# Hyena long convolution by folded half-length transforms, with the modulation sums moved to GpSimd

## The chip, the cores and the metric

The kernel runs on one core of a Trainium2 chip. The metric is the device time of one launch in microseconds; lower is better. The profile is one execution of the same program, taken by the hardware profiler.

## The reference

Two transformer-like blocks are applied to a latent sequence of 512 positions and 1024 features, all in float32. Only the first block is touched by the change. Cut to what matters:

```python
mod_x = silu(c) @ w_mod + b_mod            # 6 x 1024 values for the latent sequence
mod_c = silu(c_ctx) @ w_mod + b_mod        # the same for the context (only shift and scale are used)
hx = modulate(rmsnorm(x), sh_a, sc_a)
hc = modulate(rmsnorm(ctx), csh_a, csc_a)
q, k, v, hy = split(hx @ w_in)             # attention and Hyena inputs
attn = differential_attention(q, [k_ctx, k], [v_ctx, v])

def hyena_filters(L):                      # 2 orders x 2 directions x 512 channels
    h = MLP_with_sines(positions) * exp(-t * deltas)
    k_full = concat([h_forward, 0, reversed(h_backward[1:])])
    return rfft(k_full)                    # length 2 L

def long_conv(z, k_f):                     # circular convolution of length 2 L = 1024
    zf = rfft(z, n=2 * L)
    return irfft(zf * k_f, n=2 * L)[:L]

def hyena_mixer(proj):
    v, x1, x2 = split(short_conv(proj))
    z = v
    for n, gate in enumerate((x1, x2)):
        z = gate * (long_conv(z, k_f[n]) + skip[n] * z)
    return rmsnorm(z)

x = x + g_a * (concat([attn, hyena]) @ w_out)
x = x + g_f * conv_ffn(modulate(rmsnorm(x), sh_f, sc_f))
```

The second block follows (gated linear recurrences, cross-attention, a feed-forward part).

## The kernel before

The program is written by hand, one instruction stream per engine, with semaphores between them. Everything is held transposed, features on the 128 partitions and the 512 positions along a row. A table of jobs (`job_plan`) gives each product that TensorE makes a number; job n uses PSUM bank n mod 8, and the jobs run strictly in the order of the table. Two weight slots of 2 MB each are filled by SyncE (L515) in the order of `slab_plan`; a slot is loaded again once TensorE has finished the last job that uses it.

**Precision.** Some products run in plain float32 (L649, L750, L856, L866). Others split both operands in a high and a low part and make three cheaper products (L662 to L664, L695 to L700). For those ScalarE makes the high part of a weight slab (`split_w`, L1191), and VectorE or GpSimd the low part (`split_w`, L1756; `split_half`, L2454).

**The modulation.** The vector silu(c) @ w_mod is made in 12 slabs of 512 columns. VectorE (`mod_products`, L1802 and L1804) multiplies each of a slab's 8 row blocks with a column of silu(c) and adds them up; TensorE then sums over the partitions with a product against ones (`modulation`, L715; the job `mod_s`), and VectorE adds the bias (`mod_column`, L1815). Slabs 0 to 3 are made for both the latent and the context vector, so 16 VectorE instructions each; slabs 4 to 11 for the latent alone, 8 each. Slabs 0 to 3 are needed for the first norm, slab 4 to 11 not before the end of the attention block's output projection.

**The Hyena filters.** At the start of the program TensorE makes the filter taps (jobs h4, L735), VectorE forms the sum and the difference of the two directions (L1827 to L1837), and TensorE transforms them for each of 2 orders: 4 tiles of the real part, 4 of the imaginary part and one row for the Nyquist term, each of 4 float32 matmuls of 128 x 512 (L750, L755). ScalarE takes them out of PSUM.

**The attention** runs in 16 steps n (head n // 4, row block n % 4). In a step TensorE makes the scores (L811), the transposes of the weights of step n - 2 (L799), and in 12 of the 16 steps one Hyena input tile (L649); VectorE takes maxima (L1922), makes the weights (L1906 to L1912) and the taps of the short convolution (L1896, L1897).

**The Hyena stage** follows, once for each order o: four groups of transposes (L847), ScalarE copies them out, then the transform jobs Zre and Zim for 4 tiles m (L856, 4 matmuls each), VectorE's complex product with the filter spectrum (L1961 to L1970, six instructions per m), the inverse transform jobs y for 4 tiles c (L866, 8 matmuls of 128 x 512 each), and the skip term and gate on VectorE (L1983, L1985). The sums of modulation slabs 4 to 11 stand between these on VectorE, and their slabs pass through the weight slots. The second order's z needs the first's output. Then the output projection starts (`first_products`, L695), which waits for the low part of slab out 0 that GpSimd makes.

**GpSimd before** does little up to here: it adds the high and low parts of hx1 (L2443), reloads the transform table and the inverse table (L2427), and makes the low part of slab out 0.

Of the kernel before, what the change touches and what calls it, by code (L numbers as in the profile page):

```python
# [62 lines left out]
for _n, _w in CONSTS:  # L63
# [16 lines left out]
EARLY_MOD_AT = {"Kim_0_0": ["mod_0"], "Kim_0_3": ["mod_1"], "Kre_1_2": ["mod_2"], "Kim_1_1": ["mod_3"]}  # L80

MOD_AT = {at: [f"mod_{4 + n}"] for n, at in enumerate(
    [("Z", 0, 1), ("y", 0, 0), ("y", 0, 1), ("y", 0, 2), ("y", 0, 3), ("Z", 1, 1), ("Z", 1, 3), ("y", 1, 0)])}


def job_plan():
# [5 lines left out]
    spectra = []  # L92
    for o in range(2):
        spectra += [f"Kre_{o}_{m}" for m in range(HC)] + [f"Kim_{o}_{m}" for m in range(HC)] + [f"Knyq_{o}"]
    for n in spectra:
        j += [n] + EARLY_MOD_AT.get(n, [])
# [4 lines left out]
    for n in range(HEADS * NT + 3):  # L101
# [6 lines left out]
        if n in HY_STEPS:  # L108
            j += [f"hy_{HY_STEPS.index(n)}"]
        if n >= 2 and (n - 2) % NT == NT - 1:  # L110
            j += [f"o_{(n - 2) // NT}"]
        if n >= 3 and (n - 3) % NT == NT - 1:
            j += [f"norm_o_{(n - 3) // NT}"]
    for o in range(2):
        j += [f"zt_{o}_{t}" for t in range(NT)]
        for m in range(HC):
            j += [f"Zre_{o}_{m}", f"Zim_{o}_{m}"] + MOD_AT.get(("Z", o, m), [])
        for m in range(HC):
            j += [f"y_{o}_{m}"] + MOD_AT.get(("y", o, m), [])
    j += ["norm_hy"]  # L120
    j += [f"out_{m}" for m in range(KD)]
# [74 lines left out]
def slab_plan():  # L196
# [3 lines left out]
    s += [("mod", n, f"mod_{n}") for n in range(4, 12)]  # L200
# [48 lines left out]

def two_blocks(nc, io, out_dram):  # L250
    jobs = job_plan()
# [6 lines left out]
    with ExitStack() as ctx:  # L258
# [32 lines left out]
        eps = sb("eps", [P, 1])  # L291
        pool_note = sb("pool_note", [P, 1])
# [29 lines left out]
        Adft = words(0, 4 * 1024).rearrange("p (t f) -> p t f", t=NT)  # L322
        Bdft = tiles(8, 8)
# [3 lines left out]
        Knq = [tile(24 + 9 * o) for o in range(2)]  # L327
# [15 lines left out]
        mod_acc2 = [tile(82), tile(83)]  # L343
# [8 lines left out]
        hyt = [tile(80), tile(81)]  # L352
# [89 lines left out]

        def mod_sums(s):
# [47 lines left out]
        def _(sp):  # L491
# [6 lines left out]
            load(con[:], io["consts"], "con")  # L498
            load(xin, io["xT"].rearrange("(k p) t -> p k t", p=P), "x")
# [23 lines left out]
            load(Adft, io["dft"].rearrange("(t p) f -> p t f", p=P), "dft")  # L523
# [9 lines left out]
            for n in range(3):  # L533
                slab("hy", n, io["w_in"], 1536 + 512 * n)
            for n in range(4, 12):
                slab("mod", n, io["w_mod"], 512 * n)
            for n in range(2):
                slab("out", n, io["w_out"], 512 * n)

# [64 lines left out]
        def _(pe):  # L604
# [104 lines left out]
            def modulation(s):  # L709

                pe.wait_ge(sem("mod_summed"), s + 1)
# [1900 lines left out]
```

## Time and profile before

| | us |
|---|---|
| median of 3 runs | 2027.31 |
| lowest and highest run | 2027.23 and 2028.23 |
| the profiled execution, span from first to last instruction | 2023.3 |
| median run less that span | 4.0 |

The profiled execution has no time of its own beside its span; the 4.0 us are what a run has around the span.

| engine | busy us | share of the span | instructions |
|---|---|---|---|
| TensorE (PE) matmuls | 1875.4 | 93% | 7086 |
| VectorE (DVE) | 1013.9 | 50% | 1358 |
| ScalarE (ACT) | 661.0 | 33% | 1003 |
| GpSimd (POOL) | 162.0 | 8% | 120 |

The busy share says where an engine had work, not that it ran at its peak. A float32 matmul of the program appears as two records in the trace, so 16 matmuls of 128 x 512 are a row with x32. The chain of waits goes back from the last instruction to what released it; a stretch of TensorE in it means that nothing else was late there.

### The profile page before, as it was taken

What the parts mean: (1) busy time and instruction counts of PE and PEld (TensorE: products, weight loads), DVE (VectorE), ACT (ScalarE), POOL (GpSimd) and SP (SyncE); (2) the same over time, 40 slices, a digit from 0 to 9 for tenths busy, and PEclk for the clock granted to TensorE, in tenths of its full rate; (3) what the DMA queues carried; (4) which work ended last, traced back from release to release, by engine and by line L of the source; (5) the groups of instructions that cost most, each with busy time, mean ns of one, the idle gap of its engine ahead of it and who ended that gap; (6) DMA issues with size and microseconds to landing.
All of it is one profiled execution on the core that took longest, in us unless ns stands there. A gap on an engine that the chain in (4) does not pass through costs nothing.

```text
span 2023.3 us, 18405 instructions
## 1 busy us (share of the span) xinstructions
PE 1875.4 (93%) x7086; PEld 1282.2 (63%) x7086; DVE 1013.9 (50%) x1358; ACT 661.0 (33%) x1003; POOL 162.0 (8%) x120
## 2 busy tenths in 40 slices
PE   6999898889999999999799988898989899999997
PEld 2447544344477888888475544444777668888886
DVE  6833255558545442443437658568443435333443
ACT  4151133420124331332443243254433333223231
POOL 0000200000111000000101212213300010000001
PEclk9899899999999999999899999899989999999999
DMA  7221311034322223232222111110142122232231
GB/s 240 83 83 42 125 42 42 1 125 166 125 83 85 92 95 104 89 104 78 84 92 94 42 42 42 42 45 0 63 166 84 42 84 83 83 113 94 83 108 58
DMA packets 99617, 169.41 MB, mean 84 GB/s; under 512 B 2843, under 2 KB 38171, under 8 KB 99356
## 3 DMA queue, kind: packets, MB, share of 16 engines
q1 hardware_dynamic: 97292, 159.97, 22.9%
q0 software_dynamic: 2256, 8.52, 1.3%
q8 instruction: 44, 0.72, 0.1%
q14 instruction: 25, 0.20, 0.0%
HBM read 166.38 MB, written 2.10 MB: 83 GB/s over the span
## 4 chain that ended last, share of the span: by engine, by line
PE 82%; DVE 9%; ACT 5%; issue 2%; POOL 1%; DMA 1%; SPq 0%; DVEq 0%; ACTq 0%; POOLq 0%
PE bank L662 11%; PE bank L663 11%; PE bank L664 11%; PE bank L649 9%; PE bank L695 5%; PE bank L696 5%; PE bank L700 4%; PE bank L856 3%; PE bank L992 2%; PE bank L750 2%; PE bank L1050 2%; PE bank L866 2%; PE bank L640 2%; PE bank L811 2%; PE bank L980 1%
## 5 line engine op out<-in xcount | busy, mean ns | idle before, releaser
L649 PE MATMUL bank<-arena,weight_slots 128*128 128x512 f32 (+1 forms) x512 | 213.3, 572 | 0.0
L649 PEld LDWEIGHTS bank<-arena,weight_slots 128*128 128x128 f32 x512 | 97.3, 194 | 101.6 <-issue 100.0
L695 PE MATMUL bank<-xn_hi,weights_hi 128*128 128x512 f32 x320 | 125.7, 393 | 6.2 <-ACT xn_hi L1196 6.2
L1191 ACT ACTIVATE weights_hi<-weight_slots 128x2048 fp32r<-128x2048 f32 (+2 forms) x46 | 77.0, 1724 | 155.6 <-DMA weight_slots<-in_ffn_w_down 66.3
L2438 POOL TENSOR_TENSOR arena<-arena 128x512 f32<-128x512 f32 (+1 forms) x38 | 52.5, 1383 | 935.2 <-ACT arena L1219 932.4
L696 PE MATMUL bank<-xn_hi,weight_slots_lo 128*128 128x512 f32 x320 | 125.6, 392 | 0.0
L1180 ACT ACTIVATE arena<-bank 128x512 f32<-128x512 f32 (+2 forms) x110 | 52.7, 516 | 207.5 <-PE bank L847 63.9
L663 PE MATMUL bank<-xn_lo,weights_hi 128*128 128x512 f32 x288 | 112.1, 389 | 0.0
L662 PE MATMUL bank<-xn_hi,weights_hi 128*128 128x512 f32 x288 | 112.1, 389 | 0.0
L664 PE MATMUL bank<-xn_hi,weight_slots_lo 128*128 128x512 f32 x288 | 112.1, 389 | 0.0
L1756 DVE TENSOR_TENSOR weight_slots_lo<-weight_slots,weights_hi 128x2048 fp32r<-128x2048 f32 (+2 forms) x42 | 84.4, 2050 | 52.0 <-ACT weights_hi L1191 52.0
L2393 DVE TENSOR_TENSOR weight_slots_lo<-weight_slots,weights_hi 128x2048 fp32r<-128x2048 f32 x30 | 67.4, 2288 | 85.1 <-ACT weights_hi L1707 85.1
L1707 ACT ACTIVATE weights_hi<-weight_slots 128x2048 fp32r<-128x2048 f32 x30 | 55.8, 1909 | 161.7 <-DMA weight_slots<-in_w_up 108.8
L663 PE MATMUL bank<-sq_lo,weights_hi 128*128 128x512 f32 x256 | 99.7, 389 | 0.0
L664 PE MATMUL bank<-sq_hi,weight_slots_lo 128*128 128x512 f32 x256 | 99.7, 389 | 0.0
L662 PE MATMUL bank<-sq_hi,weights_hi 128*128 128x512 f32 x256 | 99.7, 389 | 0.0
L1219 ACT ACTIVATE arena<-arena 128x512 f32<-128x512 f32 (+1 forms) x88 | 51.0, 592 | 126.3 <-DVE arena L2410 28.4
L1804 DVE SCALAR_TENSOR_TENSOR arena<-weight_slots,silu_c,arena 128x512 f32<-128x512 f32 x112 | 81.7, 750 | 3.0
L700 PE MATMUL bank<-xn_lo,weights_hi 128*128 128x512 f32 x320 | 74.2, 389 | 0.0
L695 PEld LDWEIGHTS bank<-xn_hi,weights_hi 128*128 128x128 f32 x320 | 60.6, 189 | 20.6 <-issue 7.8
L640 PE MATMUL bank<-arena,ones 128*128 128x512 f32 (+1 forms) x72 | 39.7, 680 | 35.2 <-ACT arena L1219 34.9
L1922 DVE TENSOR_REDUCE softmax_stats<-bank 128x1 f32<-128x384 f32 x64 | 32.8, 552 | 77.4 <-PE bank L811 77.2
(363 smaller groups left out, 3852.6 us busy)
## 6 DMA issues: line engine op xcount, KB each, us to landing
weight_slots<-in_w_in SPq DMA_DIRECT2D x30, 1024.0 KB, 6.1
weight_slots<-in_w_mod SPq DMA_DIRECT2D x24, 1024.0 KB, 7.2
weight_slots<-in_ffn_w_up SPq DMA_DIRECT2D x22, 1024.0 KB, 6.5
weight_slots<-in_w_up SPq DMA_DIRECT2D x16, 1024.0 KB, 6.3
weight_slots<-in_w_down SPq DMA_DIRECT2D x16, 1024.0 KB, 6.1
weight_slots<-in_w_out SPq DMA_DIRECT2D x8, 1024.0 KB, 6.5
weight_slots<-in_w_xkv SPq DMA_DIRECT2D x8, 1024.0 KB, 6.2
weight_slots<-in_ffn_w_down SPq DMA_DIRECT2D x8, 768.0 KB, 5.4
```

Of the source, the lines that this page charges most:

```text
L640: ins = mm(ps[:, 0:width], ones[:], sq[(first + k) % 2][:, 0:width], start=k == 0, stop=k == n - 1)
L649: ins = mm(ps[:, 0:width], w[:, k, P * m:P * m + P], rhs[:, k, 0:width], start=k == 0, stop=k == kk - 1)
L662: mm(ps, lh, rh, start=start, stop=False)
L663: mm(ps, lh, rl, start=False, stop=False)
L664: return mm(ps, ll, rh, start=False, stop=stop)
L695: mm(ps[:, 0:width], wh(k, m), x2[0][:, k, 0:width], start=k == 0, stop=False)
L696: mm(ps[:, 0:width], wl(k, m), x2[0][:, k, 0:width], start=False, stop=False)
L700: ins = mm(ps[:, 0:width], wh(k, m), x2[1][:, k, 0:width], start=False, stop=k == KD - 1)
L1191: A(high(kind, n)[:, a:b], W[:, s_, a:b], ACT.Copy).then_inc(w_hi, 1)
L1756: V.tensor_tensor(W_lo[:, s, a:b], W[:, s, a:b], high(kind, n)[:, a:b].bitcast(F32), ALU.subtract).then_inc(w_lo, 1)
L1804: ins = V.scalar_tensor_tensor(acc, w[:, k, :], g, acc, ALU.mult, ALU.add)
L2393: V.tensor_tensor(W_lo[:, s % 2, a:b], W[:, s % 2, a:b], W_hi[:, s % 2, a:b].bitcast(F32), ALU.subtract).then_inc(w_lo, 1)
```

## The change

1. **Shifted frequencies.** The transform is taken at the odd frequencies of a negacyclic convolution (each half is a length-512 problem with 256 frequency pairs), so there is no Nyquist term. The filter taps are taken in the order even, odd; each of the 2 x 2 x 2 spectrum items is an even part and an odd part of 2 matmuls each (jobs KE and KO). ScalarE copies KE out, and VectorE adds and subtracts KO (`spectrum_pair`, two instructions each, 16 in all).
2. **Folded z.** VectorE adds and subtracts the mirrored halves of z (`fold`, two instructions of 128 x 256 per tile) before the transposes. A Z job has 2 matmuls where it had 4.
3. **Inverse.** A y job has 8 matmuls of 128 x 256 in the two halves of a bank, and VectorE adds and subtracts them (four instructions of 128 x 256 in place of one of 128 x 512).
4. **The complex product** is split: VectorE makes the four products per m; the sum and the difference of m = 0, 1, 2 go to GpSimd (`spectrum_sums`), those of m = 3 stay on VectorE.
5. **Modulation.** For slabs 0 to 3 VectorE makes the latent sum only and GpSimd the context sum. Slabs 4 to 11 no longer pass through the weight slots: GpSimd loads their row blocks of 128 x 512 one at a time into two buffers, scales each in place and adds it (`mod_stream`). [...] Slabs 4 to 9 run on GpSimd beside the attention; 10 stands between the two spectrum_sums, 11 behind the second. The TensorE jobs mod_4 to mod_9 stand in attention steps 4, 6, 8, 11, 13 and 15, mod_10 behind y_1_0, mod_11 behind out_7.
6. **Loads.** The tables come from SyncE (the first is 1 MB where it was 2 MB). The out slabs follow the hy slabs directly.

```diff
-EARLY_MOD_AT = {"Kim_0_0": ["mod_0"], "Kim_0_3": ["mod_1"], "Kre_1_2": ["mod_2"], "Kim_1_1": ["mod_3"]}
+SPECTRA = [(o, c, m) for o in range(2) for c in ("re", "im") for m in range(2)]
+EARLY_MOD_AT = {(0, "re", 1): 0, (0, "im", 1): 1, (1, "re", 1): 2, (1, "im", 1): 3}
+STEP_MOD = {4: 4, 6: 5, 8: 6, 11: 7, 13: 8, 15: 9}
+LATE_MOD_AT = ("y", 1, 0)
...
             def modulation(s):
-                pe.wait_ge(sem("mod_summed"), s + 1)
+                if s < 4:
+                    pe.wait_ge(sem("mod_summed"), s + 1)
+                pe.wait_ge(sem("pool_step"), (2 * KD - 1) * (s + 1))
...
+            def fold(o, c):
+                z = u[:, c, :]
...
+                V.tensor_tensor(folded[:, c, 0, :], z[:, 0:256], z[:, 511:255:-1], ALU.add).then_inc(sem("fold_done"), 1)
+                V.tensor_tensor(folded[:, c, 1, :], z[:, 0:256], z[:, 511:255:-1], ALU.subtract).then_inc(sem("fold_done"), 1)
...
+                    left, right = z[:, 255::-1], z[:, 256:512]
+                    V.scalar_tensor_tensor(right, right, skip, ps[:, 0:256], ALU.mult, ALU.add)
+                    link(V.scalar_tensor_tensor(left, left, skip, ps[:, 0:256], ALU.mult, ALU.add))
+                    V.tensor_tensor(right, right, ps[:, 256:512], ALU.add)
+                    free(V.tensor_tensor(left, left, ps[:, 256:512], ALU.subtract), name)
...
+            def settled(ins):
+                steps_made[0] += 1
+                ins.then_inc(sem("pool_step"), 1)
+                pool.wait_ge(sem("pool_step"), steps_made[0])
+            def add_scaled(acc, w, scratch, g, k):
+                if k == 0:
+                    settled(G.tensor_scalar(acc, w, g, None, ALU.mult))
+                    return
+                settled(G.tensor_scalar(scratch, w, g, None, ALU.mult))
+                settled(G.tensor_tensor(acc, acc, scratch, ALU.add))
...
+            def mod_stream(s):
+                mod_buffer_free(pool, s)
+                for k in range(KD):
+                    i = KD * (s - 4) + k
+                    pool.wait_ge(sem(f"ld_mod_row{i % 2}"), 16 * (i // 2 + 1))
+                    add_scaled(mod_sums(s)[0], mod_rows[i % 2], mod_rows[i % 2], silu[:, k, 0:1], k)
+                    if (s, k) < (11, KD - 2):
+                        mod_row(s + (k + 2) // KD, (k + 2) % KD)
...
+            pool.wait_ge(sem("rope_done"), 2 * HEADS)
+            for s in range(4, 10):
+                mod_stream(s)
...
+            spectrum_sums(0)
+            mod_stream(10)
+            spectrum_sums(1)
+            mod_stream(11)
             def split_half(kind, n, e):
...
```

The order of the instructions, at three places.

TensorE from the filter spectra (L750, L755; now L787) to the first norm's sum and the k products. Before:

```order
L750 MATMUL bank<-arena 128x512 x20
L715 MATMUL bank<-ones,arena 128x1 x8
L750 MATMUL bank<-arena 128x512 x12
L715 MATMUL bank<-ones,arena 128x1 x8
L755 MATMUL bank<-arena 1x512 x4
L750 MATMUL bank<-arena 128x512 x12
L715 MATMUL bank<-ones,arena 128x1 x8
L750 MATMUL bank<-arena 128x512 x12
L715 MATMUL bank<-ones,arena 128x1 x8
L750 MATMUL bank<-arena 128x512 x8
L755 MATMUL bank<-arena 1x512 x4
L640 MATMUL bank<-arena,ones 128x256 x8
```

Now:

```order
L787 MATMUL bank<-arena 128x512 x8
L756 MATMUL bank<-ones,arena 128x1 x8
L787 MATMUL bank<-arena 128x512 x8
L756 MATMUL bank<-ones,arena 128x1 x8
L787 MATMUL bank<-arena 128x512 x8
L756 MATMUL bank<-ones,arena 128x1 x8
L787 MATMUL bank<-arena 128x512 x8
L756 MATMUL bank<-ones,arena 128x1 x8
L679 MATMUL bank<-arena,ones 128x256 x8
```

72 matmuls have become 32; the last modulation job (L756) now stands directly ahead of the context norm's sum (L679).

TensorE in the Hyena stage, order 0 (transposes L847, Z L856, y L866). Before:

```order
L847 MATMUL bank<-consts,arena 128x128 x16
L856 MATMUL bank<-arena 128x512 x16
L715 MATMUL bank<-ones,arena 128x1 x4
L856 MATMUL bank<-arena 128x512 x16
L866 MATMUL bank<-arena 128x512 x8
L715 MATMUL bank<-ones,arena 128x1 x4
L866 MATMUL bank<-arena 128x512 x8
```

Now (transposes L881, Z L892, y L905):

```order
L881 MATMUL bank<-consts,arena 128x128 x16
L892 MATMUL bank<-arena 128x512 x16
L905 MATMUL bank<-arena 128x256 x32
```

The Z matmuls are half in number, the y matmuls half in width, and no modulation job stands between them.

GpSimd from the hx1 sums to the low part of slab out 0. Before:

```order
L2443 TENSOR_TENSOR arena<-hx_lo,hx_hi 128x512 x8
L2427 DMA arena<-in_dft 128x4x1024
L2427 DMA arena<-in_idft 128x8x512
L2454 TENSOR_TENSOR weight_slots_lo<-weight_slots,weights_hi 128x2048 x2
```

Now, the end of that stretch (spectrum_sums L2546 and L2549, mod_stream L2501 to L2518, split_half L2560):

```order
L2546 TENSOR_TENSOR arena<-arena 128x512
L2549 TENSOR_TENSOR arena<-arena 128x512
L2501 TENSOR_SCALAR arena<-arena,silu_c 128x512
L2518 DMA arena<-in_w_mod 128x512
...
L2503 TENSOR_SCALAR arena<-arena,silu_c 128x512
L2504 TENSOR_TENSOR arena<-arena 128x512
L2560 TENSOR_TENSOR weight_slots_lo<-weight_slots,weights_hi 128x2048 x2
```

The two instructions that make the low part of slab out 0 now stand behind all of mod_stream(11).

## Rows read from the trace of the kernel before

**Rows 1.** The page: its first line.

```profile
span 2023.3 us, 18405 instructions
```

**Rows 2.** The chain of waits in order of time: start us, length us, what (records).

```profile
68.38 3.57 PE bank L715 x16
131.73 27.70 PE bank L766 x64
244.31 2.94 PE bank L811 x8
409.22 6.88 PE bank L649 x16
445.73 13.86 PE bank L856 x32
537.49 22.41 PE bank L866 x48
```

**Rows 3.** Stretches, from:to length, busy us of each engine (records), PEclk, DMA share, GB/s.

```profile
313.70:318.50 4.80, 4.77 (x10) 1.71 (x10) 0.56 (x1) 1.32 (x2) 0.00 (x0) 0.50 0.01 3
459.00:499.00 40.00, 35.87 (x114) 17.99 (x113) 37.12 (x58) 2.06 (x4) 0.00 (x0) 0.96 0.52 179
```

**Rows 4.** VectorE's timeline, start us, us, [idle before <-releaser]: filters, last head norm, modulation.

```profile
56.05 0.69 DVE L1837 TENSOR_TENSOR arena<-arena 128x512 f32<-128x512 f32 x1
428.66 0.75 DVE L1749 SCALAR_TENSOR_TENSOR arena<-arena,subln_scaled,rstd 128x512 f32<-128x512 f32 x1 [10.19 <-ACT rstd L1230]
429.88 5.47 DVE L1804 SCALAR_TENSOR_TENSOR arena<-weight_slots,silu_c,arena 128x512 f32<-128x512 f32 x7
```

**Rows 5.** SyncE's timeline, and the landing of slabs up to 120 us.

```profile
71.98 16.00 SPq L515 DMA_DIRECT2D weight_slots<-in_w_mod  x4
DMA to landing us min/median/max: 5.0/7.5/19.4
```

**Rows 6.** TensorE's timeline, the context norm's sum.

```profile
127.00 4.72 PE L640 MATMUL bank<-arena,ones 128*128 128x256 f32 x16 [1.69 <-ACT arena L1219]
```

**Rows 7.** GpSimd's timeline: memset, adds in a row, a load, a lone add, the low part.

```profile
538.22 8.98 POOL L2454 TENSOR_TENSOR weight_slots_lo<-weight_slots,weights_hi 128x2048 fp32r<-128x2048 f32 x2 [107.33 <-ACT weights_hi L1191]
610.99 0.95 POOL L2465 MEMSET arena<- 128x1024 f32 x1
960.89 7.01 POOL L2438 TENSOR_TENSOR arena<-arena 128x512 f32<-128x512 f32 x5 [345.14 <-ACT arena L1219]
1314.62 0.59 POOL L2427 DMA_DIRECT2D arena<-in_tri  x1 [13.78 <-PE bank L1012]
1632.64 1.29 POOL L2438 TENSOR_TENSOR arena<-arena 128x512 f32<-128x512 f32 x1 [167.48 <-ACT arena L1219]
```

**Rows 8.** GpSimd's timeline beside the rope.

```profile
231.19 12.51 POOL L2443 TENSOR_TENSOR arena<-hx_lo,hx_hi 128x512 f32<-128x512 f32 x8 [230.21 <-PE bank L664]
```

**Rows 9.** VectorE's timeline in the same stretch.

```profile
232.80 1.43 DVE L1880 TENSOR_TENSOR arena<-arena 128x512 f32<-128x512 f32 x1
234.16 1.75 DVE L1875 TENSOR_TENSOR arena<-arena 128x512 f32<-128x512 f32 x1
235.83 0.68 DVE L1877 TENSOR_TENSOR arena<-bank,arena 128x512 f32<-128x512 f32 x1
236.61 0.97 DVE L1880 TENSOR_TENSOR arena<-arena 128x512 f32<-128x512 f32 x1
```

**Rows 10.** TensorE's timeline in the attention, behind a wait.

```profile
313.73 2.05 PE L640 MATMUL bank<-arena,ones 128*128 128x512 f32 x2 [5.54 <-ACT arena L1219]
```

**Rows 11.** VectorE's timeline: the context parts (256 wide); in the Hyena stage.

```profile
181.90 2.77 DVE L1762 TENSOR_TENSOR hc_lo<-arena,hc_hi 128x256 fp32r<-128x256 f32 x8
461.55 0.69 DVE L1970 TENSOR_TENSOR arena<-arena 128x512 f32<-128x512 f32 x1
468.26 2.49 DVE L1762 TENSOR_TENSOR mix_lo<-arena,mix_hi 128x512 fp32r<-128x512 f32 x4
```

More of the change, by code:

```diff
@@ L91, in job_plan @@
     j += [f"h4_{o}_{t}_{d}" for o in range(2) for t in range(NT) for d in range(2)]
[L92 to L96, printed above, removed]
+    for o, c, m in SPECTRA:
+        j += [f"KE{c}_{o}_{m}", f"KO{c}_{o}_{m}"]
+        if (o, c, m) in EARLY_MOD_AT:
+            j += [f"mod_{EARLY_MOD_AT[o, c, m]}"]
     j += ["norm_ctx"]
@@ L326, in two_blocks @@
         Kim = [tiles(20 + 9 * o, 4) for o in range(2)]
-        Knq = [tile(24 + 9 * o) for o in range(2)]
+        mod_rows = [tile(24), tile(33)]
         u = tiles(34, 12)
@@ L532, in _ @@
             slab("q", 0, io["w_in"], 0)
-            for n in range(3):
+            for n in range(2):
                 slab("hy", n, io["w_in"], 1536 + 512 * n)
-            for n in range(4, 12):
-                slab("mod", n, io["w_mod"], 512 * n)
+            done(sp, f"v_{V_ORDER[-1]}")
+            load(Zdft, tables["dft_z"].rearrange("(t p) f -> p t f", p=P), "dft_z")
+            slab("hy", 2, io["w_in"], 1536 + 1024)
             for n in range(2):
                 slab("out", n, io["w_out"], 512 * n)
+            done(sp, f"wt_{HEADS - 1}_{NT - 1}_1")
+            load(Bdft, tables["idft_y"].rearrange("(f p) t -> p f t", p=P), "idft")
             up_v = io["ffn_w_up"].rearrange("(k p) (a c) -> p k a c", p=P, a=2)
@@ L1845, in _ @@
                 mod_products(n)
[L1846 to L1849 removed]
+                if n:
+                    mod_column(n - 1)
+                for pair in SPECTRA[2 * n:2 * n + 2]:
+                    spectrum_pair(*pair)
+            mod_column(3)
             for n in range(4):
@@ L1946, in _ @@
                 evicted(dve, f"hy_{m}")
-            dve.wait_ge(sem("kim0"), 2)
+            for o, c, m in SPECTRA:
+                evicted(dve, f"KO{c}_{o}_{m}")
+            def fold(o, c):
+                z = u[:, c, :]
+                if o:
+                    for t in range(NT):
+                        done(dve, f"zt_0_{t}")
+                V.tensor_tensor(folded[:, c, 0, :], z[:, 0:256], z[:, 511:255:-1], ALU.add).then_inc(sem("fold_done"), 1)
+                V.tensor_tensor(folded[:, c, 1, :], z[:, 0:256], z[:, 511:255:-1], ALU.subtract).then_inc(sem("fold_done"), 1)
+            dve.wait_ge(normed, sum(norms[f"norm_o_{HEADS - 1}"]))
+            for c in range(HC):
+                fold(0, c)
             for o in range(2):
@@ L1995, in _ @@
                 head_split(k)
-            for s in range(4, 12):
+            for s in range(4, 11):
                 evicted(dve, f"mod_{s}")
```

262 lines of the change are left out of this document (144 added, 118 removed).

## The prediction

> **What bounds the kernel now.** I read the page first, then the chain of waits in order of time, then stretches, then each engine's timeline where the change touches it. The span is 2023.3 us [rows 1]; the median run is 4.0 us longer, and I carry every difference over to the median. The chain [rows 2] shows TensorE from the filter spectra to the end of the Hyena stage, with short links elsewhere: the k products start at 131.7, the attention at 244.3, its last hy tile ends at 416.1, the last y job ends at 559.9. A row of x32 there is 16 float32 matmuls in 13.9 us, so 0.87 us each. In 459 to 499 us VectorE is as full as TensorE, 37.1 and 35.9 of 40.0 us [rows 3]; so halving TensorE's work there also needs the modulation sums gone from VectorE. Early, VectorE ends the filters at 56.7, and seven multiply-adds take 5.47 us, 0.78 each [rows 4]. Slab mod 2 is issued at 72.0, when TensorE has done mod 0 (begun at 68.4, 3.57 us) [rows 2, 5], and lands 7.5 us after its issue, the second half 0.5 later. The context norm's sum takes 4.7 us [rows 6] and then the k products start. GpSimd is idle until 231 us.
>
> **What is removed from TensorE.** Spectra: 72 - 32 = 40 matmuls, 35 us. Z: 16 per order, 28 us for both. y: 32 per order at half width, by the columns 0.43 us each: again 28 us. That is 91 us of TensorE, but what counts is what is late next, and that is GpSimd.
>
> **A GpSimd slab.** An add alone takes 1.29 us; five in a row that wait for each other take 7.01, so one each 1.43 and 0.14 for the wait [rows 7]. No TENSOR_SCALAR of GpSimd is in the trace. From below it is half the memset of 1024 columns, 0.48 us; from above the add, 1.29. It reads one tensor where the memset reads none and the add two: I take the middle, 0.88. A load of a row block has 128 rows like that of tri, 0.59 us to issue [rows 7]; with the wait 0.73. A slab from the weight slots: 8 x (0.88 + 0.14) + 7 x 1.43 = 18.2 us. A streamed one has 8 loads more: 24.0 us. A load has about 3.2 us (one scale, add and issue) until its data are wanted; I take it as hidden, and if it isn't, every missing us counts eight times per slab.
>
> **Contention.** While GpSimd adds hx1, 8 instructions take 12.5 us, 1.60 each: 0.3 more than alone [rows 8]. In the same stretch VectorE's instructions with two SBUF inputs take 0.97 and 1.75 us (first 1.43) where 0.69 is the free value [rows 4, 9], on average 0.67 more; the one that reads PSUM keeps 0.68 [rows 9]. I scale the 0.67 by GpSimd's share of reading time: 0.9 in unstreamed slabs (0.60), 0.68 in streamed ones (0.46). GpSimd pays 0.3 per such VectorE instruction. The Trainium skill ("SBUF — State Buffer", Who interferes with whom) calls the shared port an exclusive lock: the second to come waits for the whole instruction. On VectorE's side the rows agree; for GpSimd it would mean 0.72 and not 0.3 per VectorE instruction, a rival below. The page "GPSIMD Engine Reference" (Engine selection) of the Trainium skill advises against this move outright: elementwise work belongs to VectorE, GpSimd being about 2x slower with two inputs, near line rate with one. Its measured loop of 512 elements, 769 ns, as an estimate for the scale would make a slab 0.9 us shorter and the sum 2.7 us better.
>
> **Early part.** GpSimd starts when slab 0 lands, at the latest 4.6 + 19.4 = 24.0 us [rows 5]; its first two slabs end about 65, unnoticed by TensorE. But beside them VectorE's filters have 16 instructions with two SBUF inputs: 16 x 0.60 = 9.7, so they end at 66.4, with the two small ones behind them at 67.1. Sum of slab 0 (latent only, 8 instructions, 6.0): 73.1. mod_0 on TensorE 3.6: 76.7. Slab 2 lands at 84.7. GpSimd then makes two slabs, 36.4, and gives up 16 x 0.3 = 4.8 to VectorE: 125.9. VectorE's own half (16 sums at 0.75 + 0.6, 8 pairs at 1.2) ends by 118 and isn't the last. TensorE ends the 32 spectrum matmuls by 115 and waits: mod_3 ends at 129.5, the norm's sum at 134.2 (before: 131.7). So none of the 35 us saved in the spectra is kept. TensorE was idle for over 10 us there. Behind an idle time of 5.5 us [rows 10] its granted clock was 0.50 for 4.8 us [rows 3], that is 1.2 and not 2.4 GHz, which costs 2.4 us. Early part: **+4.9 us**. All that follows shifts by this; times below are without it.
>
> **Attention.** Six columns of 4 small matmuls, 0.9 us each; the one in step 6 falls into an idle time like that before 313.7 [rows 10]: +4.5. The maxima's small TENSOR_TENSOR, two SBUF inputs, is exposed once a head: 4 x 0.46 = 1.8. Elsewhere the transposes ask for the weights two steps later and find them ready. **+6.3.** Slabs 4 to 9 meet five such instructions a step, some 12 per slab: 24.0 + 3.6 = 27.6 us, six make 165.6. The last is wanted at 416.1 + 5.5, so 177.3 after the start: 29.6 per slab. Covered, with 2.0 us per slab to spare.
>
> **Hyena stage.** The last head norm ends at 429.4 [rows 4] + 6.3 = 435.7. New on the path: 8 folds of 128 x 256 at 0.35 [rows 11], 2.9; the rest of the transposes and two copies, 1.6: Z starts at 440.2 (before 431.0). 16 matmuls, 14.0, and 2.4 for the low clock: 456.6. VectorE is as far as 2.65 us behind the last Z job (459.6 to 462.2 before [rows 2, 11]): Y complete at 459.3. GpSimd's last pair for m = 2 ends at 457.3, just hidden. mod_stream(10) then runs to 457.3 + 24.0 + 3.6 = 484.9. VectorE has 4 head splits (0.62 each [rows 11]) and for each c 0.41 + 0.46 + 2 x 0.35 + 0.69 + 2 x 0.35 + 0.2 = 3.2, and 0.46 for each of the 16 with two SBUF inputs: 4.3 + 18.4 = 22.7, until 482.0. TensorE needs 3.5 per c and waits for it. Z of order 1: 483.6 to 500.0, low clock again. spectrum_sums(1) can't start before 487, so slab 10 is hidden by 2 us. They end at 496.5 + 1.3 + 2.9 = 500.7.
>
> **The end of the stage.** The y jobs end about 518. But GpSimd goes 500.7 + 23.8 (slab 11; two loads fewer, four contended instructions more) = 524.5, and only then makes the low part of slab out 0, 9.0 us [rows 7]: 533.5. The output projection starts there and not at 559.9: **-26.4**, of which TensorE gives back **+2.4** for the low clock. mod_11 behind out_7 and GpSimd's two adds of the Hyena norm lie beside work or waits that are there already: 0. Sum: 4.9 - 26.4 + 2.4 = -19.1 us (the attention's 6.3 lies within): 2027.3 - 19.1 = **2008**, and a span of 2004.
>
> **The rivals.**
> (a) Cheaper scales: GpSimd's TENSOR_SCALAR at the memset's pace, 0.48. 3.2 us per slab; three slabs are on the path (2, 3 and 11): -9.6, 1999. For it: one input only; against: nothing in the trace shows it.
> (b) GpSimd loses the whole VectorE instruction, as the lock of the page would have it. Then 0.42 more for each of 16 + 4: +8.4, 2017; the attention still fits, 29.1 per slab. For it: 1.75 us on VectorE looks like a full block; against: the 0.3 of [rows 8].
> (c) The scale costs as much as the add: +3.3 per slab: 9.9, and the attention's slab is 30.9, 1.3 over its time, six times: 7.8. 2026, no change.
> (d) Slower: the stream misses its places in the attention. TensorE then waits at each mod job, and with it everything else, since the jobs are strictly in order. Each us of a slab beyond 27.6 costs 3, and beyond 29.6 another 6. That meets the whole gain at 3.45 us more and is measurably slower from 3.9 more, a slab of 31.5 us. (b) and (c) together, or loads that come half a us late each, give it: at 33.0 us, 16.2 + 20.4 - 19.1 = +17.5, 2045. For it: the margin of 2.0 us. Against: it takes two of the unknown costs at their bad end.
> That the transforms are not halved is excluded by the instruction order.
>
> **How the numbers follow.** My own sum 0.45 (2000 to 2014), (a) 0.15, (b) 0.20, (c) and what lies near it 0.09, (d) 0.11. I call no change what is within 0.2%, 4.1 us, about what a measurement of this kernel can tell. Faster: 0.45 + 0.15 + 0.20 = 0.80; same 0.09; slower 0.11. The range leaves out (d) and the far end of (a): 1994 to 2030.
>
> **What would show it.** TensorE idle before the last early L756 and before the first L734, in both cases waiting for GpSimd; the k products at 134 to 137 us; GpSimd's TENSOR_SCALAR at 0.9 and its slabs 27 to 28 us apart in the attention; VectorE's L1872 and L1873 at 1.3; no wait of TensorE for GpSimd at the six attention columns; spectra of order 1 not waiting for slab 10. I am wrong if the output projection doesn't wait for GpSimd, if the attention does, or if the part behind the output projection changes by more than 2 us.

## The result, and where the time went

The changed kernel takes **2050.56 us** in the median (2050.13 to 2052.84, 4 runs), the kernel before 2027.27 in the same session; the ratio is 1.0124, 95% interval 1.011 to 1.0139. It is slower by 1.2%. The prediction was 2008 us (1994 to 2030): wrong, in sign too, and outside its range.

The profiled execution of the changed kernel spans 2051.0 us, that of before 2023.3 [rows 1]. These are 27.7 us apart where the medians are 23.3 apart. In the four runs of the changed kernel the time is 1.8 us above the span, so the 4.0 us between median and span of before are not all what a run has around its span: by the 1.8, the profiled execution of before was 2.2 us faster than its median, and that of the changed kernel, the slowest of four, was 2.3 us slower. I divide up the 27.7. First the page of the changed kernel (span, then the busy time of the engines):

```profile
span 2051.0 us, 18300 instructions
PE 1808.1 (88%) x6942; PEld 1268.5 (62%) x6942; DVE 1003.2 (49%) x1306; ACT 653.6 (32%) x989; POOL 484.5 (24%) x374
```

The chain of waits of the changed kernel in order of time, cut to the places that [rows 2] shows of before (start, us, what):

```profile
73.13 3.57 PE bank L756 x16
...
108.21 2.86 issue
111.08 3.54 PE bank L756 x16
...
124.42 9.36 issue
133.77 3.55 PE bank L756 x16
...
143.29 27.71 PE bank L800 x64
...
255.86 2.94 PE bank L845 x8
...
486.99 3.02 PE bank L881 x13
...
577.21 8.96 POOL weight_slots_lo L2560 x2
```

The attention's last norm sum, of before and then of the changed kernel, in TensorE's timeline:

```profile
426.14 1.10 PE L640 MATMUL bank<-arena,ones 128*128 128x512 f32 x2 [1.50 <-ACT arena L1219]
```

```profile
482.58 1.10 PE L679 MATMUL bank<-arena,ones 128*128 128x512 f32 x2 [1.50 <-ACT arena L1259]
```

Four sections come out of it:

| section | before | changed | difference | predicted |
|---|---|---|---|---|
| until the k products start | 131.7 | 143.3 | +11.6 | +4.9 |
| to the last norm sum of the attention (426.1, 482.6) | 294.4 | 339.3 | **+44.9** | +6.3 |
| to the start of the output projection (559.9, 586.2) | 133.8 | 103.6 | -30.2 | -32.7 |
| the rest | | | +1.4 | +2.4 |

(The third prediction is the text's -26.4 without the attention's 6.3.) So the halved transforms and the moved sums give in the Hyena stage what they were expected to give. The attention takes it back, one and a half times.

TensorE's waits in the attention of the changed kernel, 255 to 490 us (whom it waited for: us in total, times, longest):

```profile
PE bank L688 <- DVE arena L1934: 19.5, 3, 6.9
PE bank L845 <- DVE arena L1917: 9.8, 1, 9.8
PE bank L756 <- DVE arena L1934: 6.4, 1, 6.4
PE bank L679 <- DVE arena L1934: 6.3, 1, 6.3
PE bank L688 <- DVE mod L1851: 5.3, 1, 5.3
PE bank L833 <- DVE arena L1934: 5.2, 1, 5.2
PE bank L845 <- DVE arena L1934: 4.8, 1, 4.8
PE bank L679 <- ACT arena L1259: 4.8, 2, 3.3
```

In the same view of before, 244 to 430 us, VectorE's taps (L1897 there) cost it 4.0 and 1.9 us, once each. More than by these it was held up at the four norm sums, where it waited for ScalarE's squares:

```profile
PE bank L640 <- ACT arena L1219: 18.1, 4, 5.5
```

L1934 is the second tap of a hyena channel tile on VectorE, L1851 the bias of a modulation column. Without the 9.8, which before has too, these are eight waits for VectorE of together 47.5 us (the expectations below say seven). None is for GpSimd. They are not all new: the 4.8 answers to the 4.0 of before, and the 6.3 (L679) stands where the norm sum of head 1 waited 5.55 us for ScalarE. The six others, 36.4 us, have no counterpart in before.

So the 44.9 us add up as follows. From the first scores to the last norm sum TensorE waits 53.8 us in the changed kernel (the eight waits, 4.8 for ScalarE at two norm sums and 1.5 at L868) and 24.0 us in the kernel before, 29.8 more. The 36.4 are partly paid for by the norm sums, which wait 7 us less. TensorE is busy for 172.8 us and not 157.8, 15.0 more: 6.7 are the six modulation jobs, and most of the rest are the matmuls that run slower behind the waits.

TensorE's timeline at steps 5 and 6 (start, us, what, and in brackets the idle time before it and who ended it):

```profile
303.64 0.95 PE L756 MATMUL bank<-ones,arena 128*128 128x1 f32 x8
304.52 1.57 PE L845 MATMUL bank<-arena 64*128 64x384 f32 x8
306.02 0.87 PE L833 MATMUL bank<-consts,arena 128*128 128x128 f32 x6
313.64 9.34 PE L688 MATMUL bank<-arena,weight_slots 128*128 128x512 f32 x16 [6.75 <-DVE arena L1934]
322.82 5.31 PE L868 MATMUL bank<-arena 128*128 128x512 f32 x12
...
336.81 1.83 PE L756 MATMUL bank<-ones,arena 128*128 128x1 f32 x8 [6.38 <-DVE arena L1934]
```

Two things are to be seen. The hy product of step 5 (L688) needs nothing that VectorE makes in that step; it waits for a **bank**. And 16 matmuls behind the wait take 9.34 us where undisturbed ones take 7.03: from 313.64 to 318.50 us TensorE's granted clock is 0.54 of full speed, after that 1.00, as in [rows 3, 10].

The bank follows from the list of jobs. Job number n uses PSUM bank n mod 8 and must wait until job n - 8 is evicted. Worked out from the list for the steps 4 and 5 of the attention:

```
before:   hy_3 : 2 | s s s s : 3 4 5 6 | wt wt : 7 0 | hy_4 : 1
changed:  hy_3 : 0   mod_4 : 1 | s s s s : 2 3 4 5 | wt wt : 6 7 | hy_4 : 0
```

A step has seven jobs, so the hy product of the next step lies seven on and takes another bank. With a mod job between them it lies eight on, and comes to the bank of hy_3. VectorE empties that bank with its taps of step 4, and those stand in its queue behind the maxima of step 5 and the combination of step 4. The maxima in turn wait for TensorE's scores of step 5. TensorE can run only the scores and six transposes ahead, then stands until VectorE is through. The list gives the other five new waits in the same way. The jobs hy_7 and hy_9 lie eight behind hy_6 and hy_8, with mod_6 and mod_7 between them. mod_5 lies eight behind hy_4, and hy_5 behind mod_5 (L1851). The second transposes of step 14 (L833, the 5.2) lie eight behind hy_10. In before none of them lies eight behind a job that VectorE's taps free. The norm sum of head 1 does, in both kernels alike (eight behind hy_7), so the mod jobs did not put it there. The distance alone is not yet a wait: mod_6 lies eight behind hy_5 and mod_8 behind hy_9, but a hy product of 7 us stands just before them, and they came without one. VectorE's side of the same wait:

```profile
308.88 1.24 DVE L1948 TENSOR_SCALAR arena<-arena,softmax_stats 128x768 f32<-128x768 f32 x1
310.15 1.90 DVE L1949 SCALAR_TENSOR_TENSOR arena<-arena,softmax_stats 128x768 f32<-128x768 f32 x1
311.98 0.74 DVE L1933 SCALAR_TENSOR_TENSOR arena<-bank,params,arena 128x511 f32<-128x511 f32 x1
312.75 0.75 DVE L1934 SCALAR_TENSOR_TENSOR arena<-bank,params,arena 128x511 f32<-128x511 f32 x1
...
329.08 2.06 DVE L1959 TENSOR_REDUCE softmax_stats<-bank 128x1 f32<-128x384 f32 x4 [15.51 <-PE bank L845]
```

Behind the taps VectorE itself idles 15.5 us: the two engines take turns. But the rows show a second suspect. The combination, L1948 and L1949, takes 1.24 and 1.90 us; free it takes 0.62 and 1.02. So two theories went to the chip: **banks** (the place of the mod jobs) and **port** (GpSimd's stream slows VectorE).

### The profile page after: what moved, and what is told of

Same layout as the page of the kernel before. It is cut to its first block, busy times and chain, and to the rows that moved or that the text cites. A ratio compares the mean times of both kernels' runs of the same rounds, so it can differ in the third digit from the quotient of the medians.

```text
span 2051.0 us, 18300 instructions
## 1 busy us (share of the span) xinstructions
PE 1808.1 (88%) x6942; PEld 1268.5 (62%) x6942; DVE 1003.2 (49%) x1306; ACT 653.6 (32%) x989; POOL 484.5 (24%) x374
## 4 chain that ended last, share of the span: by engine, by line
PE 77%; DVE 11%; ACT 4%; issue 3%; POOL 3%; DMA 1%; DVEq 0%; SPq 0%; ACTq 0%; POOLq 0%
PE bank L701 11%; PE bank L702 11%; PE bank L703 11%; PE bank L688 10%; PE bank L734 5%; PE bank L735 5%; PE bank L739 4%; PE bank L1032 2%; PE bank L679 2%; PE bank L1090 2%; PE bank L1020 2%; PE bank L845 1%; PE bank L892 1%; PE bank L800 1%; DVE arena L1829 1%
## 5 line engine op out<-in xcount | busy, mean ns | idle before, releaser
L688 PE MATMUL bank<-arena,weight_slots 128*128 128x512 f32 (+1 forms) x512 | 222.9, 592 | 24.9 <-DVE arena L1934 19.5
L688 PEld LDWEIGHTS bank<-arena,weight_slots 128*128 128x128 f32 x512 | 100.4, 200 | 133.4 <-issue 113.0
L2504 POOL TENSOR_TENSOR arena<-arena 128x512 f32<-128x512 f32 x84 | 112.2, 1336 | 7.0
L1220 ACT ACTIVATE arena<-bank 128x512 f32<-128x512 f32 (+2 forms) x102 | 48.0, 510 | 195.8 <-PE bank L787 61.7
L2597 POOL TENSOR_TENSOR arena<-arena 128x1024 f32<-128x1024 f32 x18 | 54.4, 3024 | 172.3 <-ACT arena L1523 172.3
L2503 POOL TENSOR_SCALAR arena<-arena,silu_c 128x512 f32<-128x512 f32 x56 | 90.6, 1617 | 5.3 <-DMA arena<-in_w_mod 2.8
```

Source lines behind the costliest of these rows:

```text
L688: ins = mm(ps[:, 0:width], w[:, k, P * m:P * m + P], rhs[:, k, 0:width], start=k == 0, stop=k == kk - 1)
L2503: settled(G.tensor_scalar(scratch, w, g, None, ALU.mult))
L2504: settled(G.tensor_tensor(acc, acc, scratch, ALU.add))
```

## The experiments

Gains are given below against the changed kernel, as the difference of the two ratios to the kernel before times 2027 us, since the sessions differ by a us or two. The changed kernel stands at 1.0124.

### The attention: bank or port

**late_columns.** The jobs mod_4 to mod_9 leave the attention:

```diff
-        if n in STEP_MOD:
-            j += [f"mod_{STEP_MOD[n]}"]
...
+    j += [f"mod_{s}" for s in range(4, 10)]
     for o in range(2):
         j += [f"zt_{o}_{t}" for t in range(NT)]
```

> The changed kernel with the TensorE jobs mod_4 to mod_9 taken out of the attention and put behind it; GpSimd's stream runs as before and doesn't wait for them (so the columns 4 to 7 come from later sums). Theory 'banks': a mod job takes the next of the eight PSUM banks, and then the hy product of the following step, or the next mod or norm job, comes to the bank that VectorE frees only behind the combination of the step; seven waits of 4.8 to 6.9 us, 47.5 in all. Without the jobs they go: 2012 us (2005 to 2022). Theory 'port': VectorE is slowed by the stream, and this does not change: 2045 to 2050.

Measured: 2020.1 us, ratio 0.9969 (0.9959 to 0.998), so -31.4 us. The place of the jobs, as 'banks' has it, and not the port. From the first scores to the last norm sum the attention takes 187.8 us, in the changed kernel 226.7, in before 181.8.

**narrow_stream.** The stream stays but hardly touches the SBUF; the sums of slabs 4 to 9 are left out but for their first term:

```diff
+                if narrow and k:
+                    acc, w, scratch = acc[:, 0:4], w[:, 0:4], scratch[:, 0:4]
```

> The changed kernel with the stream's instructions of slabs 4 to 9 on 4 columns and not 512, but for the first of each slab (loads, jobs and waits as they are; the sums of these slabs are left out). Theory 'port': VectorE is free of GpSimd in the attention, 45 us go: 2005 to 2010. Theory 'banks': the seven waits stay, each some 1.5 us shorter since VectorE's combination is: 2036 to 2043.

Measured: 2043.3 us, ratio 1.0072 (1.005 to 1.0095): -10.5 us, at the upper end of the 'banks' range. VectorE's combination is back at 1.02 us (mean of L1949), and the waits are still there, only shorter:

```profile
PE bank L688 <- DVE arena L1934: 14.7, 3, 5.0
...
PE bank L833 <- DVE arena L1934: 5.2, 1, 5.2
PE bank L756 <- DVE arena L1934: 5.0, 1, 5.0
PE bank L845 <- DVE arena L1934: 4.0, 1, 4.0
PE bank L688 <- DVE mod L1851: 3.5, 1, 3.5
```

**late_and_narrow.** Both edits.

> Both of the edits before: jobs behind the attention and the stream on 4 columns. Both theories: the attention is as long as in the kernel before, 45 us shorter: 2003 us (1998 to 2010). 'Banks': about 5 to 9 us below late_columns. 'Port': as narrow_stream, within 4 us.

Measured: 2008.9 us, ratio 0.9915 (0.9893 to 0.9936): -42.4. It lies 11 us below late_columns, where 'banks' had 5 to 9. The attention takes 179.8 us, 2.0 less than in before. The four kernels make a table, and it is additive:

| ratio | jobs in the attention | jobs behind it |
|---|---|---|
| stream of 512 columns | 1.0124 | 0.9969 |
| stream of 4 columns | 1.0072 | 0.9915 |

The place of the jobs costs 31 to 32 us, the port 10 to 11, 42.4 together. That is close to the 44.9 us by which the attention had grown, though the two are not the same measure: the six mod jobs themselves (0.95 us each, undisturbed) are in all four kernels. "The port" stands here for all that the width of GpSimd's instructions does; with 4 columns they are also shorter.

**empty_jobs.** The same mechanism put into the kernel *before*, where nothing else of the change is:

```diff
+EMPTY_STEPS = (4, 6, 8, 11, 13, 15)
...
+                if n in EMPTY_STEPS:
+                    ps = begin(f"empty_{n}")
+                    for m in range(4):
+                        ins = mm(ps[:, m:m + 1], ident, ones[:, 0:1], start=True, stop=True)
+                    end(ins)
```

> The kernel BEFORE with six empty TensorE jobs (four one-column matmuls, a result of four columns that nothing uses) in the steps 4, 6, 8, 11, 13 and 15 of the attention, where the change has its mod jobs; VectorE frees their bank behind the taps. No GpSimd work, no sums. Theory 'banks': the place alone makes TensorE wait as in narrow_stream against late_and_narrow, 34 us, and the jobs themselves take 5.7: 2027 + 40 = 2067 us (2058 to 2074). Theory 'port': only the jobs, 2033 us (2030 to 2036).

Measured: 2058.8 us, ratio 1.0167 (1.0148 to 1.0187), +33.9 us for six jobs whose matmuls take some 6 us and that compute nothing. The expected 40 were too much by 6, the 'port' figure of 2033 is excluded. Less the jobs themselves, their place costs 28 us here. TensorE's waits in its attention, 244 to 480 us, are nearly line for line those of narrow_stream:

```profile
PE bank L655 <- DVE arena L1908: 14.7, 3, 5.0
...
PE bank L805 <- DVE arena L1908: 5.2, 1, 5.2
PE bank L832 <- DVE arena L1908: 4.9, 1, 4.9
PE bank L817 <- DVE arena L1908: 4.0, 1, 4.0
PE bank L655 <- DVE empty_note L1954: 3.5, 1, 3.5
```

**guest_columns.** The mend. The transposed weights fill 384 of the 512 columns of their bank, and the column matmuls go into the rest, without a job of their own; ScalarE copies them out before it frees the bank:

```diff
+                    s_ = STEP_MOD.get(NT * h + t + 2)
+                    if n == 1 and s_:
+                        pe.wait_ge(sem("pool_step"), ...)
+                        for m in range(4):
+                            ins = mm(ps[:, 384 + m:385 + m], mod_sums(s_)[0][:, P * m:P * m + P], ones[:, 0:1], start=True, stop=True)
```

> The changed kernel, output as wanted, with the columns of slabs 4 to 9 as guests in the unused 128 columns of the banks of the transposed weights (steps 5, 7, 9, 12, 14, 17); ScalarE copies the four columns out, VectorE adds the biases once. No job and no bank is added in the attention. Theory 'banks': as late_columns, without the 6 us of mod jobs behind the attention and with a short wait for slab 9: 2016 us (2011 to 2024). If it is the late sums or the column jobs themselves that held TensorE, no better than 2040.

Measured: 2024.6 us, ratio 0.9995 (0.9978 to 1.0011): -26.2, just beyond the end of what I expected. The attention ends 26.7 us earlier (the first transposes of the Hyena stage at 460.31, not 486.99). The waits for the taps are gone but for two, the 6.3 of the norm sum of head 1 and the 4.8, which no mod job had caused. This one is new:

```profile
PE bank L838 <- POOL arena L2509: 10.3, 1, 10.3
```

That is rival (d) of the prediction, at one place of six: in the shorter attention the stream of 30 to 31 us a slab is too slow, and slab 9 comes 10.3 us late, though its columns are asked for two steps later than in the change.

### The early part and the price of the scale

GpSimd's instructions in the changed kernel, 60 to 560 us, by form (count, busy us, mean ns, idle before):

```profile
L2504 POOL TENSOR_TENSOR arena<-arena 128x512 f32<-128x512 f32 x70 | 93.4, 1335 | 5.8
L2503 POOL TENSOR_SCALAR arena<-arena,silu_c 128x512 f32<-128x512 f32 x52 | 84.2, 1620 | 5.1 <-DMA arena<-in_w_mod 2.8
L2518 POOL DMA_DIRECT2D arena<-in_w_mod x61 | 36.5, 598 | 17.8 <-POOL arena L2504 15.4 <-POOL arena L2501 2.4
L2503 POOL TENSOR_SCALAR arena<-weight_slots,silu_c 128x512 f32<-128x512 f32 x19 | 33.0, 1738 | 1.9
```

The scale is **dearer** than the add, 1.62 and 1.74 us against 1.34, and not between a memset and the add as I had bounded it (0.48 to 1.29). Undisturbed it takes 1.56 to 1.57, the add 1.26. The slabs 2 and 3 took GpSimd from 85.6 to 133.7, 48.1 us where I had 41.2.

**ctx_all_vector.** The context halves of slabs 0 to 3 back on VectorE:

```diff
-            for s in range(4):
+            for s in ():
                 n = slabs["mod", s][0]
                 pool.wait_ge(w_landed[n % 2], 32 * (n // 2 + 1))
```

> The changed kernel with the context halves of slabs 0 to 3 back on VectorE, as in the kernel before; all else as changed. Theory 'GpSimd is the last early': VectorE makes its sums uncontended, 11.7 us a slab: mod_0 at 68.4, slab 3 summed at about 113, the k products start at 119 to 125 (changed: 143.3; before: 131.7), 2050.6 - 22 = 2029 us (2024 to 2034). If TensorE or the loads are late instead, the k products stay above 135 and the time above 2042.

Measured: 2022.3 us, ratio 0.9985 (0.9975 to 0.9995): -28.2, better than the 22 (2024 to 2034) that I expected. The k products start at 118.39, 24.9 us earlier, and the Hyena stage's first transposes 26.7 earlier. So the halved spectra do shorten the early part, by 13.3 us against before, once GpSimd is out of it: of the 35 us saved in matmuls the change as made kept none and added 11.6.

**scale_two_input.** The scale as a two-input multiplication, with the silu column repeated:

```diff
-                settled(G.tensor_scalar(scratch, w, g, None, ALU.mult))
+                settled(G.tensor_tensor(scratch, w, g.to_broadcast([P, 512]), ALU.mult))
```

> The changed kernel with GpSimd's scale written as a TENSOR_TENSOR with the silu column repeated over the 512 columns, in place of the TENSOR_SCALAR of 1.57 us. If the multiplication of two tensors costs what the add costs (1.26), a slab is 2.4 us shorter, three slabs lie on the path (2, 3 and 11): 2050.6 - 7 = 2043 us (2039 to 2047). If it is the multiplication and not the form that is dear, or the repeated column costs more, no change or slower.

Measured: 2053.3 us, ratio 1.0126 (1.0108 to 1.0145): no gain where I had 7 us, though the multiplication took 1.05 us and mod_3 came at 126.90 and not 133.77. The attention started 6.2 us earlier (249.62) and ended 3.6 later (first transposes at 490.56). It was 9.8 us longer. Of these 7.5 are matmuls that took longer (TensorE busy for 181.4 us and not 173.9), with a granted clock of 0.81 against 0.85 in the same stretch. What moved the clock this run doesn't show; the same edit comes again in three_two_input.

### The end of the Hyena stage

TensorE at the output projection of the changed kernel:

```profile
586.20 0.80 PE L734 MATMUL bank<-mix_hi,weights_hi 128*128 128x512 f32 x1 [21.61 <-POOL weight_slots_lo L2560]
```

**split_first.** Nobody wants slab 11 before the feed-forward network, so it goes behind what the projection waits for:

```diff
             spectrum_sums(1)
-            mod_stream(11)
 ...
             add_squares("norm_hy")
+            mod_stream(11)
             add_squares("norm_ffn")
```

> The changed kernel with mod_stream(11) of GpSimd moved behind the low parts of slab out 0 and the two sums of squares of the Hyena norm. If the output projection waits for GpSimd's serial order only (21.6 us in the trace), 19 to 21 us go: 2030 us (2028 to 2034). If the Hyena norm or the y jobs were as late, less than 10 us go.

Measured: 2022.7 us, ratio 0.999 (0.9977 to 1.0003): -27.2, more than the 19 to 21 I expected. The wait has gone, and the projection starts at full clock:

```profile
560.95 0.58 PE L734 MATMUL bank<-mix_hi,weights_hi 128*128 128x512 f32 x1
561.36 0.39 PE L735 MATMUL bank<-mix_hi,weight_slots_lo 128*128 128x512 f32 x1
```

Behind the wait of the changed kernel the matmuls there took 0.63 us each for the first 5 us. The projection's start moved by 25.2 us: the 21.6 of the wait, and 3.3 by which this execution's attention ended earlier (first transposes at 483.73), which the edit doesn't explain. The clock gives 1.4 more up to the first feed-forward products (635.27 and 661.89). So the edit itself is worth some 23 us. The profiled executions lie 32.3 us apart, 5 more than the medians. The rest of the 32.3 is the attention's 3.3 and 5.5 us that arise behind 1240 us (3.9 of them by 1302), where both kernels do the same, and that I have not traced.

### The transforms alone, and the three mends together

**transforms_alone.** Folded transforms, every modulation sum on VectorE with its slab in the weight slots and its job between Z and y as before; GpSimd keeps only the spectrum sums.

```diff
-            for s in range(4, 10):
-                mod_stream(s)
...
+                mod_products(4 if o == 0 else 9)
                 for m in range(HC):
```

> The folded transforms alone: all modulation sums on VectorE, their slabs in the weight slots and their jobs between the Z and y jobs, as in the kernel before; GpSimd keeps only the spectrum sums. My sum: early 119 to 125 in place of 131.7; attention as before; in the Hyena stage VectorE had 88.2 us of work in 129 us and now has 88.2 + 5.6 (folds) + 14 (y) - 8.3 (sums on GpSimd) = 99.5, and the stage takes 104 to 112: 2027.3 - 10 - 21 = 1996 us (1988 to 2008). If the VectorE order makes the halved transforms useless (the reason given for moving the sums away), the stage stays at 125 to 129 us and the time at 2012 to 2020.

Measured: 1991.6 us, ratio 0.9823 (0.9807 to 0.984), **1.8% faster than before and 3.0% than the change**. The Hyena stage takes 112.2 us (414.35 to 526.54), before 132.8. TensorE now waits there for VectorE's sums. Over the whole execution (us, times, longest):

```profile
PE bank L758 <- DVE arena L1831: 41.5, 10, 13.1
```

Four of these waits, 19.9 us, are the early ones (the longest is that before mod_0); the six others, 21.6 us, lie in the Hyena stage.

That is the premise on which I accepted the move to GpSimd ("halving TensorE's work there also needs the modulation sums gone from VectorE" [rows 3]): half right. VectorE does become what TensorE waits for, but 20 us were to be had before that.

**three_mended.** ctx_all_vector, guest_columns and split_first in one kernel.

> The changed kernel with three edits together, output as wanted: context halves on VectorE (alone -28.3 us), guest columns (-26), slab out 0 split before the stream of slab 11 (-28). If they lie on the path one behind the other: 2050.6 - 82 = 1968 us (1962 to 1980). If they share time (one wait hides behind another): above 1985.

Measured: 1972.3 us, ratio 0.9735 (0.9719 to 0.9751): -78.9 against the change, where the three alone give 28.2 + 26.2 + 27.2 = 81.6. They lie nearly one behind the other.

**three_two_input.** The same with the scale of scale_two_input.

> three_mended with GpSimd's scale as a two-input multiplication, 1.05 us in place of 1.57. The wait for slab 9 at the end of the attention (10.3 us in guest_columns) goes, the VectorE combinations get some longer: 1961 us (1955 to 1968). If the contention or TensorE's clock takes all of it back, as when this edit was made alone: within 4 us of three_mended.

Measured: 1988.9 us, ratio 0.9817 (0.9798 to 0.9836): **16.6 us slower** than three_mended, on both theories a miss. The combinations of VectorE in the attention, first in three_mended, then in three_two_input (count, busy us, mean ns):

```profile
L1958 DVE SCALAR_TENSOR_TENSOR arena<-arena,softmax_stats 128x768 f32<-128x768 f32 x16 | 22.4, 1398 | 0.6
L1957 DVE TENSOR_SCALAR arena<-arena,softmax_stats 128x768 f32<-128x768 f32 x16 | 14.1, 884 | 0.6
```

```profile
L1958 DVE SCALAR_TENSOR_TENSOR arena<-arena,softmax_stats 128x768 f32<-128x768 f32 x16 | 27.2, 1703 | 0.6
L1957 DVE TENSOR_SCALAR arena<-arena,softmax_stats 128x768 f32<-128x768 f32 x16 | 19.2, 1200 | 0.6
L1954 DVE TENSOR_TENSOR softmax_stats<-softmax_stats,lam 128x1 f32<-128x1 f32 x16 | 11.6, 723 | 0.5
```

Over the attention and its edges (226 to 428 us) VectorE is busy for 137.7 us and not 114.5. Each multiplication is 0.5 us shorter, and VectorE is busy for 23 us more. The attention takes no less (228.55 to 433.12, and 230.53 to 435.51), although the wait for slab 9 is gone: what that gave went into VectorE's combinations and so into TensorE's waits behind them (for VectorE's second tap 11.1 us before, 29.1 now). The granted clock was no lower here (0.89, and 0.87 in three_mended), so a lower clock isn't what this edit must bring. The Hyena stage is 5 us longer (76.6 and 81.7 us to the output projection), and 2.0 had arisen before the attention. That accounts for 7.5 us up to the projection (509.73 and 517.22). The difference is 9.9 at the first feed-forward products (584.60 and 594.48) and 13.4 at 973.83 and 987.24; why it grows there, where both do the same, stays open, and so does the cause of the 5 and the 2 us.

**ninth_later.** three_mended with slab 9's column as a job of its own behind the third pair of Z jobs of order 0, where it repeats no bank at the wrong time.

```diff
+            if (o, m) == (0, 2):
+                j += ["mod_9"]
```

> three_mended with the columns of slab 9 not as a guest in step 17 but as a job of its own between the Z jobs of order 0. There TensorE waited 9.7 us for GpSimd and then ran at half its clock (12 matmuls in 8.3 us in place of 5.4). Expected: 12.5 us less, 1960 us (1956 to 1965). If spectrum_sums(0) behind the stream is then what is late: 1968 or more.

Measured: **1963.3 us**, ratio 0.968 (0.9652 to 0.9707): 3.2% faster than before, the best of all here. Against three_mended the ratio falls by 0.0055, 11.1 us (the medians, from two sessions, by 9.0), where I had 12.5. From the first scores to the first transposes of the Hyena stage ninth_later takes 190.6 us and not 204.6, 14.0 less. The attention began 2.5 us later, for a reason not traced, and the Hyena stage with the new job in it takes 78.9 us and not 76.6.

## Why the prediction was wrong

**The failed step** is "Attention": "Six columns of 4 small matmuls, 0.9 us each ... Elsewhere the transposes ask for the weights two steps later and find them ready. +6.3." The 0.9 us were right (0.95). What was left out is that a job also takes a bank of eight, and that the steps before had seven jobs. I had the order of the jobs and the rule of eight in front of me and costed the jobs by their duration only. What it brought were six waits of TensorE for a bank (36.4 us) and a slower clock behind them. Value of the omission: 31 us by late_columns, 32 by the pair narrow_stream and late_and_narrow, and 28 by empty_jobs in the kernel before, without the jobs' own time.

**The port in the attention** (predicted 1.8 us of exposed time) was 10 to 11. I had only the maxima's small instruction on the path; but where TensorE waits for the taps, the whole combination is on it. The mean of L1949 was 1.45 us, and 1.02 free.

**The early part**: +11.6 for +4.9. The mis-sized term is the scale, 1.62 to 1.74 us for 0.88, outside the bounds I had taken from the nearest rows. The instruction with one tensor input is not cheaper here than the one with two (1.56 and 1.26 us undisturbed). That mod_0 came at 73.13, where I had 73.1, proves nothing: the filters ended at 63.5 and not 67.1, and the seven multiply-adds of slab 0 took 8.72 us where I had left them at their free pace [rows 4]. Two errors cancelled. GpSimd's waits for the row blocks were small (2.8 us in all before the 52 streamed scales up to 560 us), so the loads were hidden as I had taken them.

**The Hyena stage**: -30.2 for -32.7, the step that held. The projection waited 21.6 us for GpSimd, where my times leave 15.5 (518 to 533.5). The chain was as told: Z of order 0, head splits, Z of order 1, spectrum sums, slab 11, low part of slab out 0, projection. TensorE's clock behind its waits was as in [rows 3, 10].

**The rivals.** (d) had the time (2045) and not the mechanism. Its condition was met, a slab took 30 to 31 us where 29.6 were allowed, but no mod job waited for its sums: they ended at 286.0, 317.1, 346.9 and 377.7, and the jobs came at 303.6, 336.8, 366.9 and 413.9, since the attention had already been stretched by the banks. When that was mended (guest_columns), (d) appeared with 10.3 us. (c), "the scale costs as much as the add", was the nearest of the unknown costs and still too low. (b) and the lock: GpSimd's add went from 1.26 to 1.49 or 1.79 beside VectorE's filters and sums, 0.2 to 0.5 more, so not the whole VectorE instruction. One reading in (b) does not follow from my own numbers: 12 instructions per slab at 0.42 us more make a slab of 32.6 us and not 29.1, so by them the attention would not have fitted. And the 0.67 us of the contention is 0.69 by the three instructions of [rows 9], which changes little.

The Trainium skill's advice against this move ("GPSIMD Engine Reference", Engine selection: elementwise work is VectorE's) I had quoted and then given no chance of its own. ctx_all_vector and transforms_alone agree with it in this kernel; but three_mended, with eight slabs on GpSimd, beats transforms_alone by 18 us (up to the Hyena stage's first transposes its attention is 18.4 us longer, its Hyena stage 35.6 shorter), so it isn't a rule without exception.

## What to carry to other kernels

Where jobs take buffers in turn, a new job is costed by what it does to the distance between the old ones: list, for some steps, which job each one now follows in its buffer, and where that one is freed. An engine's queue that is in strict order hides a tiny job's price in the job eight places on. And an instruction that becomes shorter on GpSimd need not make the kernel faster (three_two_input): price an instruction on GpSimd by its duration and by what it takes from VectorE.

## What was not expected of the hardware

- GpSimd's TENSOR_SCALAR of 128x512 float32 with one scalar per partition takes 1.56 to 1.57 us undisturbed (the changed kernel, 112 to 133 us); TENSOR_TENSOR add 1.26; TENSOR_TENSOR multiplication by a repeated column 1.05 (mean in three_two_input).
- A VectorE instruction of two columns can take as long as a whole GpSimd instruction beside it. In three_mended, VectorE and then GpSimd (the add that it met):

```profile
270.96 1.26 DVE L1971 TENSOR_SCALAR softmax_stats<-softmax_stats 128x2 f32<-128x2 f32 x1
```

```profile
270.93 1.26 POOL L2512 TENSOR_TENSOR arena<-arena 128x512 f32<-128x512 f32 x1
```

  That instruction takes 0.17 us alone (172 ns is its mean in narrow_stream). It agrees with the lock of the Trainium skill ("SBUF — State Buffer", Who interferes with whom) as far as VectorE is the one that comes second. The same section of the Trainium skill exempts a VectorE instruction with one SBUF input unless it is in a 2-port mode, which a tensor_scalar can enter. Whether this one was in such a mode no run here shows.
- The form of GpSimd's instruction matters more to VectorE than its length: with 1.05 us of two-input multiplication in place of 1.57 us of TENSOR_SCALAR, VectorE was busy 23 us longer over the attention (three_two_input). Why, no run here shows.
- GpSimd idles 0.30 us between an instruction and the issue of a DMA that must follow it, and the issue itself takes 0.58 to 0.59. With both, a row block took 3.85 us undisturbed (257.8 to 269.3 us of the changed kernel).
